# Router logits and gathered rows made from x, and feed-forward stages whose products are scaled by 1/rms afterwards, in a two-block transformer kernel on one core

## The reference

```python
# first block (shifts and scales come from c)
h = rmsnorm(x, norm_mix) * (1 + sc1) + sh1
x = x + g1 * diff_attention(h, ...)
h = rmsnorm(x, norm_ffn) * (1 + sc2) + sh2
x = x + g2 * hier_moe(h, ...)        # router: 4 groups x 4 experts, top 2
x = rmsnorm(x, norm_final)
# hier_moe: logits h @ w_rg + b_rg and h @ w_re + b_re, group by argmax, two experts by top-k,
#           y = sum over the chosen experts of gate * (silu(t @ w_gate) * (t @ w_up)) @ w_down
# second block, for each of two layers
x = x + mixer(rms_norm(x, g_mixer))
h = rms_norm(x, ffn_norm[layer])
u = causal_dwconv(h @ w_up, conv_w, conv_b)      # 3 taps, 5632 channels
gate, val = split(u)
x = x + (silu(gate) * val) @ w_down
```

## Time and profile before

| what | value |
| --- | --- |
| median of three runs | 1876.02 us (1875.77 to 1877.65) |
| the profiled execution's own time | 1874.39 us |
| its span, first to last instruction | 1872.6 us |
| mean granted TensorE clock | 0.984 |
| PE busy | 1811.0 us (97%) |
| DVE busy | 1181.4 us (63%) |
| ACT busy | 911.4 us (49%) |
| POOL busy | 186.3 us (10%) |

### The profile page before, as it was taken

How to read it: one execution, slowest core, us unless ns; L and a number is a source line. 1 busy time by engine, 2 the same in 40 slices (tenths; PEclk the granted TensorE clock), 3 DMA queues, 4 the chain that set the end, 5 groups by cost and what they waited for, 6 DMA issues and landing times.

```text
span 1872.6 us, 26081 instructions
## 1 busy us (share of the span) xinstructions
PE 1811.0 (97%) x8508; PEld 1404.5 (75%) x8508; DVE 1181.4 (63%) x1829; ACT 911.4 (49%) x1389; POOL 186.3 (10%) x219
## 2 busy tenths in 40 slices
PE   7999999899999799999999999999998999999999
PEld 5777677788888567666788888887774778888887
DVE  6777785789898573454566665224998466566422
ACT  3566641578888534554444444115664444444220
POOL 0000000122322100001000000000774000000000
PEclk9999998799999989999999999999999999999999
DMA  9523141999999441111233233321210222322321
GB/s 400 185 95 97 57 148 67 325 363 376 378 375 367 171 180 51 46 34 35 79 102 100 90 101 104 99 99 45 68 67 34 79 68 94 103 94 90 118 95 56
DMA packets 72786, 259.21 MB, mean 138 GB/s; under 512 B 10256, under 2 KB 10384, under 8 KB 71440
## 3 DMA queue, kind: packets, MB, share of 16 engines
q1 hardware_dynamic: 67536, 247.85, 37.6%
q0 software_dynamic: 4608, 8.40, 1.2%
q10 hardware_dynamic: 576, 2.10, 0.3%
HBM read 254.11 MB, written 12.58 MB: 142 GB/s over the span
## 4 chain that ended last, share of the span: by engine, by line
PE 85%; DVE 6%; issue 4%; ACT 2%; DMA 2%; DVEq 0%; SPq 0%; POOL 0%; ACTq 0%; POOLq 0%
PE ps L970 19%; PE ps L972 18%; PE ps L971 18%; PE ps L1168 3%; PE ps L1170 3%; PE ps L1169 3%; PE ps L946 2%; PE ps L1031 2%; PE ps L1188 1%; PE ps L1190 1%; PE ps L1189 1%; PE ps L1052 1%; DMA raw<-in_w_a 1%; PE ps L1380 1%; PE ps L934 1%
## 5 line engine op out<-in xcount | busy, mean ns | idle before, releaser
L970 PE MATMUL ps<-h_hi,w_hi 128*128 128x512 f32 x1184 | 473.3, 400 | 0.2 <-DVE x L2100 0.2
L972 PE MATMUL ps<-h_hi,w_lo 128*128 128x512 f32 x1184 | 461.6, 390 | 0.0
L971 PE MATMUL ps<-h_lo,w_hi 128*128 128x512 f32 x1184 | 461.2, 390 | 0.0
L124 DVE TENSOR_TENSOR w_lo<-raw,w_hi 128x1024 fp32r<-128x1024 f32 x212 | 266.2, 1259 | 192.8 <-ACT w_hi L119 187.7
L119 ACT ACTIVATE w_hi<-raw 128x1024 fp32r<-128x1024 f32 x212 | 221.4, 1049 | 204.5 <-PE ps L972 168.6
L970 PEld LDWEIGHTS ps<-h_hi,w_hi 128*128 128x128 f32 x1184 | 222.3, 188 | 74.6 <-issue 30.9
L972 PEld LDWEIGHTS ps<-h_hi,w_lo 128*128 128x128 f32 x1184 | 222.2, 188 | 47.2
L971 PEld LDWEIGHTS ps<-h_lo,w_hi 128*128 128x128 f32 x1184 | 222.4, 188 | 46.5 <-issue 2.9
L2124 DVE SCALAR_TENSOR_TENSOR tmp<-ps,param,tmp 128x511 f32<-128x511 f32 (+1 forms) x176 | 131.8, 749 | 133.5 <-ACT tmp L854 121.5
L163 DVE TENSOR_TENSOR w_lo<-ring,w_hi 128x1024 fp32r<-128x1024 f32 x128 | 149.8, 1218 | 30.4 <-ACT w_hi L159 30.2
L854 ACT ACTIVATE tmp<-ps,param 128x512 f32<-128x512 f32 x88 | 68.5, 779 | 179.5 <-PE ps L972 179.5
(11 more groups left out here) (320 smaller groups left out, 2772.9 us busy)
## 6 DMA issues: line engine op xcount, KB each, us to landing
ring<-in_w_m SPq DMA_DIRECT2D x192, 512.0 KB, 5.6
raw<-in_w_b SPq DMA_DIRECT2D x180, 512.0 KB, 3.5
raw<-in_w_a SPq DMA_DIRECT2D x32, 512.0 KB, 3.7
ada_late<-in_ada_b SPq DMA_DIRECT2D x32, 512.0 KB, 4.4
ada<-in_ada_a SPq DMA_DIRECT2D x8, 1024.0 KB, 20.8
y_tok<-y_dram SPq DMA_DIRECT2D x8, 512.0 KB, 6.7
x<-in_x SPq DMA_DIRECT2D x2, 1024.0 KB, 6.9
h_dram<-h_tok ACTq DMA_DIRECT2D x4, 512.0 KB, 3.3
```

What stands on the lines that cost most here:

```text
L124: dve.tensor_tensor(self.lo[:, s, :], self.raw[:, s, :], self.hi[:, s, :].bitcast(F32), ALU.subtract).then_inc(self.lo_done, 1)
L970: pe.matmul(dst, hi, a_hi, start=first, stop=False, skip_group_check=True)
L971: pe.matmul(dst, hi, a_lo, start=False, stop=False, skip_group_check=True)
L972: return pe.matmul(dst, lo, a_hi, start=False, stop=last, skip_group_check=True)
```

## The change

1. The adaptive shift times the router weights is summed on DVE (`wr_part`, `wr_sum`), spread over the partitions by one matmul, and added to the router bias (`router_c`). The router weights are multiplied by scale2 in place.
2. PE makes the logits from raw x (`logits`), and turns x to token rows by a matmul with a diagonal of scale2 (`turn_scaled`, `gain_diag`). Both lie, for seven of the eight chunks and the first two token blocks, between the output products m = 4 to 7 (`of_raw`). PE then adds std times the shift to the rows (`add_shift`), and ACT multiplies by 1/rms while it copies (`r_tok`).
3. The shift goes to DRAM and back as a row on every partition; these two DMAs and the four stores of h_tok are issued by SP. POOL's memsets come earlier.
4. The position matmuls are five instead of fourteen; the number of rounds is computed ahead of the gates.
5. `turn_tokens` of the first expert stands behind the sixth of eight slot pairs, and DVE makes the first w_lo and e_lo among the last pairs.
6. For both feed-forward stages h_hi and h_lo are x times the feature's gain (`gained_hi`, `gained_lo`), made chunk by chunk during the projection ahead. The norm's statistics run inside `two_products`. 1/rms is copied to SBUF (`r_kept`), and DVE multiplies each product in its bank by it before ACT's tap0 reads it (`z_done`).
7. `project` reads c_hi and c_lo, new buffers where act_out was, and writes banks 4 and 5. h32 is gone.

```diff
-                h32 = sb("h32", [P, KC, T], stack=st2)
+                sb("h_tok_at", [P, KC, T], stack=st2)
...
+            sp.wait_ge(late_done, 2 * KC)
+            sp.dma_start(s_dram.rearrange("o (p k) -> p (o k)", k=KC), mod[:, 3 * KC:4 * KC]).then_inc(shift_in, 16)
+            sp.wait_ge(shift_in, 16)
+            sp.dma_start(shift_read[:], s_dram.broadcast_to([P, D])).then_inc(shift_in, 16)
+            for t in range(NT):
+                sp.wait_ge(h_tok_done, t + 1)
+                sp.dma_start(h_dram[t * P:(t + 1) * P], h_tok[:, t]).then_inc(h_stored, 16)
...
+            def gained_hi(k, f, ready):
+                act.wait_ge(x_new, ready + k + 1)
+                act.activation(h_hi[:, k], x[:, k], ACT.Copy, scale=PR("ffn_norm", f * KC + k, 1)).then_inc(hhi_done, 1)
...
+            def gain_diagonals():
+                act.wait_ge(mod_done, KC + 1)
+                for k in range(KC):
+                    act.activation(gain_diag[k], C("ident"), ACT.Copy, scale=scale2[:, k:k + 1]).then_inc(gain_diag_done, 1)
+
+            def shift_by_chunks():
+                act.wait_ge(shift_in, 32)
+                act.activation(shift_rows[:].rearrange("q (k p) -> q k p", k=KC), shift_read[:].rearrange("q (p k) -> q k p", k=KC),
+                               ACT.Copy).then_inc(shift_done, 1)
+
+            split_and_square(sa, 6, 0, KC - AHEAD, 1, 0, 2, {3: gain_diagonals, 6: shift_by_chunks})
...
+            act.wait_ge(std_done, 2)
+            for t in range(NT):
+                act.activation(std_of[:, t], std, ACT.Copy, scale=C("pick", t * P, 1)).then_inc(std_split, 1)
             act.activation(scrap[:, 1:2], ones[:, 0:1], ACT.Exp)
+            act.wait_ge(rstd_done, 2)
             for t in range(NT):
                 act.wait_ge(h_turned, t + 1)
-                act.activation(h_tok[:, t].rearrange("p (b c) -> p b c", b=2), ps[:, t % 2 * 2:t % 2 * 2 + 2], ACT.Copy)\
-                   .then_inc(h_tok_done, 1)
-                act.wait_ge(h_tok_done, t + 1)
-                act.dma_start(h_dram[t * P:(t + 1) * P], h_tok[:, t]).then_inc(h_stored, 16)
-                if t < 2:
-                    act.wait_ge(route_sel, t + 1)
-                    act.activation((r44[:, 1], r4[:, 9])[t], (r44[:, 0], r4[:, 8])[t], ACT.Exp).then_inc(route_exp, 1)
+                act.activation(h_tok[:, t].rearrange("p (b c) -> p b c", b=2), ps[:, turned_at(t):turned_at(t) + 2], ACT.Copy,
+                               scale=r_tok[:, t:t + 1]).then_inc(h_tok_done, 1)
+                if t in (1, 2):
+                    act.wait_ge(route_sel, t)
+                    act.activation((r44[:, 1], r4[:, 9])[t - 1], (r44[:, 0], r4[:, 8])[t - 1], ACT.Exp).then_inc(route_exp, 1)
...
-                hi_parts(t_at)
...
-                        sb_.multiplied(act, it + i0, c0 + c)
+                        act.wait_ge(z_done, it * 4 + (f * 2 * FC + c + 1))
...
+            def logits(k):
+
+                for t in range(NT):
+                    last = pe.matmul(ps[:, RB, t * (NG + NE):(t + 1) * (NG + NE)], x[:, k, t * P:(t + 1) * P], w_r[:, k],
+                                     start=(k == 0 and t == 0), stop=(k == KC - 1), skip_group_check=True)
+                if k == KC - 1:
+                    last.then_inc(router_mm, 1)
+
+            def of_raw(k):
+                logits(k)
+                turn_scaled(k, 0)
+                turn_scaled(k, 1)
+
+            def turn_scaled(k, t):
+
+                return pe.matmul(ps[:, turned_at(t) + k // 4, k % 4 * P:(k % 4 + 1) * P], x[:, k, t * P:(t + 1) * P],
+                                 gain_diag[k], start=(k % 4 == 0), stop=False, skip_group_check=True)
...
+                    if m == 2 and k == 0:
+                        pe.wait_ge(wr_step, 2)
+                        pe.matmul(ps[:, 0, 0:NG + NE], ones[:], wr_sum, start=True, stop=True, skip_group_check=True)\
+                            .then_inc(bias_mm, 1)
+                    if m == 4 and k == 3:
+                        pe.wait_ge(in_param, 48)
+                        pe.wait_ge(wr_step, 4)
+                        pe.wait_ge(gain_diag_done, KC)
+                        for j in range(3):
+                            of_raw(j)
+                    if m >= 4 and k == 4:
+                        rms_sum(1, m - 1)
+                        of_raw(m - 1)
                 last.then_inc(sa.used, 1)
-                rms_sum(1, m - 2)
-
-            rms_sums(1, first=KC - 2)
-            pe.wait_ge(in_param, 48)
+                if m < 4:
+                    rms_sum(1, m - 2)
+                    if m == 3:
+                        rms_sum(1, 2)
+
+            pe.wait_ge(x_new, KC)
+            logits(KC - 1)
+            rms_sum(1, KC - 1)
+            for t in range(2):
+                turn_scaled(KC - 1, t)
+            for k in range(KC // 2):
+                turn_scaled(k, 2)
+            pe.wait_ge(std_done, 2)
+            pe.matmul(ps[:, SSQ, R_AT:R_AT + NT], std, C("pick").rearrange("p (t c) -> p t c", t=NT)[:, :, 0], start=True,
+                      stop=True, skip_group_check=True).then_inc(rb_done, 1)
+            for k in range(KC // 2, KC):
+                turn_scaled(k, 2)
+            pe.wait_ge(shift_done, 1)
+
+            def add_shift(t):
+                pe.wait_ge(std_split, t + 1)
+                for b in range(2):
+                    last = pe.matmul(ps[:, turned_at(t) + b], std_of[:, t], shift_rows[:, b * T:(b + 1) * T], start=False,
+                                     stop=True, skip_group_check=True)
+                last.then_inc(h_turned, 1)
+
+            add_shift(0)
+            add_shift(1)
+            pe.wait_ge(route_sel, 3)
+            pe.matmul(ps[:, RB, 0:NT * NE], C("before"), r16[:, 0], start=True, stop=False, skip_group_check=True)
+            for d in range(1, NT + 1):
+                last = pe.matmul(ps[:, RB, d * NE:(NT + 1) * NE], ones[:], r16[:, 0, 0:NT + 1 - d], start=False,
+                                 stop=(d == NT), skip_group_check=True)
+            last.then_inc(router_mm, 1)
+            add_shift(2)
...
+            pe.wait_ge(h_tok_done, 1)
             for k in range(KC):
...
+                turn_scaled(k, 3)
+            add_shift(3)
...
+                with pe.Fori(1, 6) as m:
+                    slots_of(m)
                 turn_tokens(r * (NE // 2), n, 0)
+                with pe.Fori(6, NE // 2) as m:
+                    slots_of(m)
...
-                two_products(i, c0, 0, lambda k: h_at if h_at + k >= 3 * KC else None)
+                two_products(i, c0, 4, lambda k: h_at, src=(c_hi, c_lo))
...
-                rms_sums(n, first=KC - 2)
+                def statistics(k):
+                    if k == 3:
+                        rms_sum(n, KC - 2)
+                        rms_sum(n, KC - 1)
+                    if k == KC - 1:
+                        pe.wait_ge(rstd_done, n + 1)
+                        spread(rstd, RB)
...
-                two_products(i0, c0, 0, lambda k: h_at)
+                pe.wait_ge(x_new, (3 if f == 0 else 5) * KC + KC - 1)
+                two_products(i0, c0, 0, lambda k: h_at, between=statistics)
...
+            dve.tensor_tensor(wr_part, w_r[:], mod[:, 3 * KC:4 * KC].unsqueeze(2).broadcast_to([P, KC, NG + NE]), ALU.mult)\
+               .then_inc(wr_step, 1)
+            dve.wait_ge(wr_step, 1)
+            dve.tensor_reduce(out=wr_sum, in_=wr_part.rearrange("p k n -> p n k"), axis=AX.X, op=ALU.add).then_inc(wr_step, 1)
...
+                if m == 3:
+                    dve.wait_ge(bias_mm, 1)
+                    dve.tensor_tensor(router_c, ps[:, 0, 0:NG + NE], PR("router_b"), ALU.add).then_inc(wr_step, 1)
+                if m == 2:
                     dve.wait_ge(late_done, 3 * KC)
                     dve.scalar_tensor_tensor(out=scale2[:], in0=mod[:, 4 * KC:5 * KC], scalar=1.0, in1=PR("norm_ffn"),
                                              op0=ALU.add, op1=ALU.mult).then_inc(mod_done, 1)
                     dve.wait_ge(mod_done, KC + 1)
+                    dve.tensor_tensor(w_r[:], w_r[:], scale2[:].unsqueeze(2).broadcast_to([P, KC, NG + NE]), ALU.mult)\
+                       .then_inc(wr_step, 1)
...
+                base = r * (12 * NE)
+                with dve.Fori(2, 6) as m:
                     slots_of(m)
+                slots_of(6)
+                sm.split_lo(dve, base, 0)
+                slots_of(7)
+                expert_tokens_lo(r * NE)
+                for c in range(1, 4):
+                    sm.split_lo(dve, base, c)
...
+            def gained_lo(k, f, h_at):
+                dve.wait_ge(hhi_done, h_at + k + 1)
+                dve.scalar_tensor_tensor(out=h_lo[:, k], in0=x[:, k], scalar=PR("ffn_norm", f * KC + k, 1),
+                                         in1=h_hi[:, k].bitcast(F32), op0=ALU.mult, op1=ALU.subtract).then_inc(hlo_done, 1)
...
+                dve.sem_inc(t_done, KC)
                 dve.wait_ge(rb_done, n + 1)
```

(4 more changed lines are left out.)

146 lines of the change are left out of this document (70 added, 76 removed).

## The result

| | before | changed |
| --- | --- | --- |
| median, us | 1875.89 (4 runs, 1874.1 to 1877.65) | 1865.01 (4 runs, 1863.2 to 1867.12) |
| profiled execution, its span, us | 1874.39, 1872.6 | 1867.12, 1865.3 |
| granted clock, mean | 0.984 | 0.985 |

The ratio is 0.9937, 95% interval [0.9922, 0.9951]: 10.9 us faster by the medians, 11.8 by the ratio. The forecast was 1861.0 in a range of 1855.5 to 1868; the range held, and 4 of the forecast's 15.0 us are missing. The profiled execution was the slowest of its four and shows 7.3.

What follows compares the result with a forecast made beforehand. TensorE (PE) was taken as the bound, 85% of what ended last, nearly all in the split products. Seams 11.8 plus router 3.2 made 15.0 us, so a median of 1861.0, range 1855.5 to 1868.

Steps and rivals of the forecast that it cites:

- Seams: Last projection product to first up product, before both feed-forward stages: 5.9 us gained each, 11.8 for both.
- Up loops: The 88 new DVE multiplies in the feed-forward up loops: cost zero, with 1.8 us of slack per pair.
- its threshold: In the up loops, DVE sets the pace once the multiply lasts 1.6 us.
- rival E: DVE sets the up loops' pace; with multiplies of 2 us each the time is about 1881; chance 0.04.
- Router: Attention output products through routing and slots: 3.9 us gained at full clock, 3.2 taken.
- Added work before E: PE's new router work ahead of the last output product's end: that end comes 10.4 us later.
- E to the last logits operation: Router, from the end of the last output product: the last logits operation starts 4.4 us later.
- One-hot: Routing chain: first one-hot 12.4 us behind the logits operation, against 11.37 before; 1.0 lost.
- One-hot to the first product: Slots, to the first expert product: 19.7 us, against 22.28 before; 2.6 gained.
- The queues: h_tok stores moved from ACT's queue to SP's: cost zero; a gather 1 us late would move the first product.
- rival B: Half clock from the end of the last output product on: 1865.1 us; chance 0.18.
- rival C: Full clock kept through the slots: 4 us more gained, 1857; chance 0.10.

Runs made afterwards that it cites:

- +0.6 us: Changed kernel plus a second multiply of the same bank into an unused buffer per up chunk: ratio to the kernel before 0.9953, 3.0 us over the changed kernel's.
- the experiment: Changed kernel with turn_tokens put back behind all eight slot pairs: ratio to the kernel before 0.9947, 1.9 us over the changed kernel's.
- the exponentials early: Changed kernel with both routing exponentials on ACT behind the second h_tok copy: ratio to the kernel before 0.9939.
- early increments: Changed kernel with initial increments of conv_done and glo_done ahead of DVE's eviction loop: ratio to the kernel before 0.9924, 2.4 us under the changed kernel's.
- the router alone: Changed kernel with its feed-forward half undone: ratio to the kernel before 0.9993, 1.3 us faster than before.
- two more operations: Changed kernel plus a second multiply and a reduction per up chunk on DVE: ratio to the kernel before 1.0126, 35.5 us over the changed kernel's.
- the four moves: Changed kernel, conv_done/glo_done increments and both exponentials earlier, last tile's turns and t = 1 turns moved into PE waits: ratio to before 0.9901, 6.8 us under changed.

## Why the prediction was right, and where 4 us went

**Seams: 11.8 forecast, 10.6 found.** The mechanism was right. The schedule behind it (late square, rstd and spread in time, two sums and a spread inside two_products at 1.8 us) held at both. The missing 1.2 us is a wait that the step did not look for: ahead of two_products `ffn_pe` still waits for conv_done, whose initial increment stood on DVE's queue behind work that the change itself had put there. Shown by moving it.

**Projection: a term that was missing.** Moving its operands to c_hi was put at nothing, without a word. It costs 1.1 us (192 products, 0.006 to 0.007 each). The trace of before did have the sign: products on gv_hi at 233 ns beside 227 on h_hi.

**Up loops: cost zero, found zero.** And its threshold was right too: no cost in the loops at +0.6 us, DVE-bound at +1.2. This was rival E, and it was about one operation away. Its price was mis-summed: by the prediction's own rule a multiply of 2 us costs 2 x 0.4 x 44 = 35 us, some 1896 and not 1881; with 1.9 us in effect 1901.7 was measured.

**Router: 3.2 forecast, 1.8 found (2.1 by the means).** The steps added up to 3.9, and 0.7 was taken off for a tail partly at half clock. That tail ran at 1.00 in the trace, so the 1.8 stand against 3.9. By its steps:
- Added work before E: 10.4 forecast, 11.2 found. of_raw was 1.34 us as forecast, seven times; the wait for x[2]'s square was 0.59, not 0.5; the bias matmul and the changes of kind between large and small matmuls took 0.4 together, where 0.7 was given. What was left out are two rms sums. Before, five of the eight stand ahead of E and three behind it; in the changed kernel seven and one. The two cost 0.36 us each, 0.7 together. The prediction took them off behind E and did not add them ahead of it. PE's rows, before (two sums behind E, merged) and after (one of them, between output products):

```profile
296.25 0.64 PE L934 MATMUL ps<-tmp,ones 128*32 128x128 f32 x16
```

```profile
275.05 0.43 PE L980 MATMUL ps<-tmp,ones 128*32 128x128 f32 x8 [0.59 <-ACT tmp L511]
```

- E to the last logits operation: 4.4 forecast, 4.6 found. Logits to selection: 4.8 and 4.8.
- One-hot: logits + 12.4 forecast, + 13.45 found. Two terms were mis-sized: add_shift(2) takes 1.8 us, not 1.0, and the register load 1.6, not 1.2. The 1.0 came from a row of 512-column float32 matmuls whose form reads 64*128, 1.99 us for eight records. The new ones read 128*128, and four records take 1.96. The trace of before had that form too, in the unread matmuls, at nearly twice the price:

```profile
914.51 3.60 PE L946 MATMUL ps<-const 128*128 128x512 f32 x8
```

- One-hot to the first product: 19.7 forecast, 19.73 found, through the earlier turn (1.8 us by the experiment). The wait for e_x ahead of that turn, 0.96 us, was not in the working, so that the sum came out to 0.03 us is luck; in the other five traces it is 18.3 to 19.1.
- The queues were costed at zero, with the warning that a later gather would move the first product. As built that held; with the exponentials early it became the next limit, at once.

**The clock.** Neither of its rivals came: the tail ran at 1.00 up to 327 and at 0.50 from 328 to 351, so half clock from E on (rival B) and full clock through the slots (rival C) are both out in this trace. In the experiments with early increments, the router alone and two more operations, the clock also fell for some 4 us in 320 to 326, and there the one-hot came 14.5 to 15.1 us behind the last logits operation, not 13.45. What the text did not reckon with is that executions of the same code differ in where the clock falls. The windows table of the changed kernel and of the one with early increments shows it in stretches that the edit does not touch:

```profile
715.00:724.00 9.00, 9.00 (x40) 6.80 (x40) 3.23 (x4) 2.12 (x3) 0.00 (x0) 0.81 0.19 58
...
1434.00:1441.00 7.00, 6.75 (x56) 2.84 (x54) 4.73 (x8) 3.98 (x7) 0.00 (x0) 0.77 0.01 4
```

```profile
715.00:724.00 9.00, 9.00 (x49) 6.52 (x47) 3.23 (x4) 2.12 (x3) 0.00 (x0) 1.00 0.15 58
...
1434.00:1441.00 7.00, 6.65 (x74) 2.83 (x73) 3.96 (x7) 4.81 (x9) 0.00 (x0) 1.00 0.00 1
```

Aligned on their matmuls, the two executions drift apart by 1.6 us in the first stretch and by 3.4 in 1428 to 1441. Of the 3.4, half is the clock. The other half only gives back what the execution with early increments had lost just before, where its own clock fell (0.79 over 1412 to 1420): the changed kernel waits for DVE at 1431.83 and the other does not, so its fall cost nothing in the end. Net of that the second stretch is worth 1.7 us. The prediction placed the median by adding 1.6 us to the profile of before; such an offset is as large as the terms argued over. The terms above account for 3.7 of the missing 4 us by the traces; the medians, with an interval of 2.7 us either way, cannot show an agreement that close.

Left open: what in a buffer's address sets the pace of a product, what makes the clock fall in the attention in one execution and not in another (PE is late there by 1.3 to 3.5 us in all thirteen traces behind that of before, those with the old router too), and how much of the four moves' 6.8 us is measurement.

## What to carry to other kernels

When work is inserted on a queue, look at every increment behind it, initial ones too: a semaphore that only says "free" still waits its turn. Price a matmul from a row with the same form (64*128 is not 128*128). When a sum is cut at a mark, here the end of the last output product, list everything that crosses the mark, old work too, and not only what is new. When a wait is removed, ask what was due just behind it (here the last store and its gather); moving work into PE's idle stretches and clearing that next limit together gave what the single move did not.

## What the runs showed of the hardware

- Products with the same shape and clock came every 0.227 us on h_hi, 0.229 on gv_hi when it starts 32 bytes past a multiple of 128, and 0.233 with it on such a multiple or 96 bytes past one, where h_hi starts too (offsets by the kernel's list of buffers; the traces hold no addresses). The offset alone does not explain it; 32 bytes of padding were worth 5.6 us of 1865.
- The granted clock stayed at 0.50 in 336 to 344 while PE showed 8.00 of 8.00 us busy with slot and unread matmuls. The Trainium skill, TensorE: Matmul & The Clock Gate, section "The HAM clock gate (the "warmup" mystery)", says that sustained activity releases the throttled state; this run does not bear that out for busy time as the profile counts it.
- In the execution of before the attention ran at a granted clock of 1.00 over 204 to 240; in that of the changed kernel at 0.95, and it was 1.6 us late from then on. Two experiments that leave the attention and the router as before show the same fall at the same place.
